# A two-block layer kernel on one core: a reordered start, with small first loads, eight alternating conversions and splits, and the norm's sum one slot later

## The chip, the cores and the metric

The kernel runs on one core of a Trainium2 chip. The metric is device time in microseconds (us) of one execution. A launch computes two neural layers, one after the other, for 256 positions with 2048 channels, all in 32-bit floating point.

## What is computed

The first block is a hybrid layer (attention and a state-space branch side by side, then a gated feed-forward part); the second is another hybrid layer with adaptive modulation. What matters for this change is the beginning of the first block:

```
def rms_norm(x, w):
    xf = x.astype(jnp.float32)
    y = xf * lax.rsqrt(jnp.mean(xf * xf, axis=-1, keepdims=True) + EPS)
    return (y * w.astype(jnp.float32)).astype(x.dtype)

def hybrid_layer(x, norm1_w, w_in, ...):
    h = rms_norm(x, norm1_w)
    proj = h @ w_in
    q, k, v, z, xbc, dt_raw = jnp.split(proj, SPLIT_POINTS, axis=-1)
    ...
    xbc = jax.nn.silu(causal_dwconv(xbc, ssm_conv_w, ssm_conv_b))
    dt = jax.nn.softplus(dt_raw.astype(jnp.float32) + dt_bias.astype(jnp.float32))
```

The kernel does not divide by the root of the mean before the product. It multiplies `X * norm1_w` by `w_in`, and the reciprocal root, one number for each position, is applied to the product afterwards. So the norm's sum of squares is not needed before the first group of output columns is finished.

## The kernel before

**Products.** Each 32-bit product is made of three TensorE passes in a reduced type: both operands are split into a high part (a rounded copy) and a low part (the remainder), and `hi*hi + hi*lo + lo*hi` is accumulated. For the activations `X` the parts are `gh` and `gl`; for the weights they are `whi` and `wlo`. ScalarE (ACT) makes the high parts, VectorE (DVE) the low parts.

**Units and slots.** The weights come as 528 units of 512 KB, each two contraction tiles by 512 output columns. A unit is loaded by the SyncE (SP) queue into one of `RAW = 8` buffers `raw`, `split(blk, j)` on ACT copies it to one of `SPLIT = 4` buffers `whi`, `split` on DVE subtracts it into `wlo`, and TensorE (PE) spends 24 matmuls of 256 columns on it (8 tiles by 3 passes). Eight units make one group of 512 output columns. The first projection `B_IN` has 88 units. Its main loop counts slots n = 0 to 87: in slot n, PE multiplies unit n, while ACT and DVE run `split(B_IN, LEAD + n)` with `LEAD = 4`, four units ahead, and then `slot1(n)`, which holds all the other work of that slot.

**The waits of a split.** `split` on ACT waits for the unit's load (`s_raw`) and until PE has finished the unit four earlier (`s_used`), because there are four `whi` buffers. `split` on DVE waits for `whi` (`s_hi`). PE waits for `wlo` (`s_lo`). SP refills a `raw` buffer when DVE has split it (`s_lo`).

**Before slot 0.** SP issues five parts of `X` (256, 256, 512, 512, 512 KB) alternating with units 0 to 4, then units 5 to 7. ACT issues the parameter table `prm` (553 columns) and the constants `cst` (ones, identity, triangle), and then, for each of eight steps u, converts two tiles of `X` (`gh`, scaled by `norm1`), and for u below 4 also splits unit u. DVE follows with `gl` and `wlo`. ACT issues `wdt` (the weights of dt) after step 1 and `mask` after step 2. PE runs 13 matmuls on zeroed data, which touch no result, and then starts unit 0 when `wlo` of it is there.

**The norm's sum.** In slots 0 to 3, `squares` on ACT squares four tiles of `X` each, into two buffers; `sum_chunk` on DVE adds the second buffer into the first, so the third and the fourth square wait for the addition before them (`s_sum`). `fold` adds the four tiles to one. In slot 7 PE sums over the channels (`sum_squares`), ACT takes the root (`root`), DVE its reciprocal (`inverse_root`), and DVE scales the first finished group out of PSUM (`ssm_evac`). Slots 8 to 14 then hold the convolution of that group: a base on ACT (`ssm_base`), three taps on DVE for each of four tiles (`ssm_taps`), and `ssm_silu` on ACT. Slots 10 to 22 hold also the steps of dt (`dt_steps`), whose last product on PE is in slot 22.

Of the kernel before, what the change touches and what calls it, by code (L numbers as in the profile page):

```python
# [18 lines left out]
ACT = mybir.ActivationFunctionType  # L19
AX_X = mybir.AxisListType.X  # L20

P = 128
# [43 lines left out]


GAINS = (15, 17, 18, 19, 20, 21, 22, 23, 25, 26, 27, 28)
FINAL = ((4, 1), (5, 1), (6, 2), (8, 2), (10, 2))
# [13 lines left out]
def build(nc, xT, weights, w_dt, w_ada, c_rows, params, const1, const2, rows, outT):  # L83
    ctx = ExitStack()
    with ctx:
# [162 lines left out]
        s_inv, s_rq, s_kb, s_rqc = sem("s_inv"), sem("s_rq"), sem("s_kb"), sem("s_rqc")  # L248
        s_rcl = sem("s_rcl")
        s_tile, s_part = sem("s_tile"), sem("s_part")  # L250
        s_fold, s_own, s_near, s_far = sem("s_fold"), sem("s_own"), sem("s_near"), sem("s_far")
# [53 lines left out]
        def _(act):  # L305
# [54 lines left out]

            act.dma_start(prm[:, :], params).then_inc(s_prm, 16)
            act.dma_start(cst[:, :], const1[:, 0:3 * P + 32]).then_inc(s_cst, 16)
            act.wait_ge(s_prm, 16)
            act.activation(small[:, 240:241], col("eps"), ACT.Copy).then_inc(s_warm, 1)

            for u in range(DT // 2):
                for c in range(len(X_PARTS)):
                    if X_PARTS[c][0] == 2 * u:
                        act.wait_ge(s_x[c], 16)
                for t in (2 * u, 2 * u + 1):  # L370
                    act.activation(gh[:, t, :], X[:, t, :], ACT.Copy, scale=col("norm1", t)).then_inc(s_gh, 1)
                if u < 4:
                    split(B_IN, u)
                if u == 1:
                    act.dma_start(wdt[:, :, :], w_dt).then_inc(s_wdt, 16)
                if u == 2:
                    act.dma_start(mask[:, :], const1[:, 3 * P + 32:]).then_inc(s_mask, 16)
# [77 lines left out]
            def slot1(n):  # L455
                if n < 4:
                    squares(0, n, SQX1)
                if n == 7:
                    root(0, D)
                g, j = n // 8 - 1, n % 8  # L460
                if 0 <= g < 3:
                    if j < 4:
                        ssm_base(g, j)
                    if j == 6:
                        ssm_silu(g)
# [43 lines left out]
                attention_slot(n, ATT0, 0, 8, 0)  # L509

            for n in range(IN_SLOTS):
                split(B_IN, LEAD + n)
                slot1(n)
# [145 lines left out]
        def _(dve):  # L659
# [71 lines left out]
            for u in range(DT // 2):  # L731
                for t in (2 * u, 2 * u + 1):
                    dve.wait_ge(s_gh, t + 1)
                    dve.scalar_tensor_tensor(gl[:, t, :], X[:, t, :], col("norm1", t), gh[:, t, :].bitcast(F32),
                                             ALU.mult, ALU.subtract).then_inc(s_gl, 1)
                if u < 4:
                    split(B_IN, u)
            dve.memset(U[:, :, 0:3], 0.0).then_inc(s_ready, 1)
# [225 lines left out]
            def slot1(n):  # L964
# [4 lines left out]
                if n == 5:  # L969
                    dve.wait_ge(s_wdt, 16)  # L970
                    dve.tensor_tensor(wdt[:, :, :], wdt[:, :, :], col("norm1", 0, DT).unsqueeze(2).to_broadcast([P, DT, 32]),
                                      ALU.mult).then_inc(s_wdtn, 1)
                g, j = n // 8 - 1, n % 8
                if 0 <= g < 3 and 1 <= j < 5:
                    ssm_taps(g, j - 1)
                dt_steps(n)
# [41 lines left out]
            for n in range(IN_SLOTS):  # L1018
                split(B_IN, LEAD + n)
                if n == 64:  # L1020
                    dve.wait_ge(s_mask, 16)
                if n == 7:
                    inverse_root(0)
                    dve.wait_ge(s_rb, 1)
                    dve.wait_ge(s_ready, 1)
                if n % 8 == 7:
                    if n < 24:
                        ssm_evac(n // 8)
                    else:
                        land(n // 8)  # L1030
                slot1(n)
# [263 lines left out]
        def _(pe):  # L1295
            def product(b, out, tiles, first, last, hi, lo, apart=False, ready=None):
# [14 lines left out]
                mm.then_inc(s_used, 1)  # L1311

            def product_high_first(out, need):

# [86 lines left out]
            def stream_in(blk, grp, n, need):  # L1401

                g, u = n // 8, n % 8
                if u == 0:
                    pe.wait_ge(s_evac, grp + g + 1)
                pe.wait_ge(s_lo, 8 * blk + n + 1)
                if g in (NAT if blk == B_IN else NAT2):
                    product_nat(n % SPLIT, (grp + g) % 2, (2 * u, 2 * u + 1), u == 0, u == 7)
                    return
                if blk == B_IN2 and n == 0:  # L1410
                    product_high_first(acc_tiles(grp % 2), need)
                    return
                product(n % SPLIT, acc_tiles((grp + g) % 2), (2 * u, 2 * u + 1), u == 0, u == 7, gh, gl,
                        ready=need if g == 0 else None)
# [18 lines left out]
            pe.wait_ge(s_zero, 1)  # L1433
            for _ in range(13):
                pe.matmul(PS[:, 7, 0:S], VS1[:, 0, 0, :], VS1[:, 0, :, :], start=True, stop=True)
# [90 lines left out]
            def slot1(n):  # L1526
                if n == 7:
                    pe.wait_ge(s_cst, 16)
                    sum_squares(0, SQX1)
# [249 lines left out]
```

## Time and profile before

| | |
|---|---|
| time, median of 3 runs | 1556.51 us (1551.45 to 1557.78) |
| profiled execution, its own time | 1558.2 us |
| span of the profiled execution | 1556.5 us |
| PE busy | 1542.8 us (99%) |
| PE weight loads busy | 1501.8 us (96%) |
| DVE busy | 1136.7 us (73%) |
| ACT busy | 779.7 us (50%) |
| mean granted TensorE clock | 0.995 |

The own time of the profiled execution is 1.7 us over its span; the span is counted from the first to the last instruction. Times in the rows are microseconds from the start of the span. The rows that the prediction reads are in the section below.

### The profile page before, as it was taken

Reading aid. Unit: us, or ns where it says so; the run is one execution under the profiler, and the core shown is the slowest. Engines: PE = TensorE matmul, PEld = TensorE weight load, DVE = VectorE, ACT = ScalarE, POOL = GpSimd, SP = SyncE. Lnnn points to the kernel's source line nnn. Section 1 sums busy time; section 2 is a strip of 40 time slices with the busy share of each in tenths; the row PEclk is TensorE's granted clock in tenths of the full one; section 3 lists DMA queues with packets and bytes.
Section 4 is the critical chain, followed back from the end, with each engine's and each line's share of the span. In section 5 each row is a group of like instructions: output and inputs, shape, how many; then the busy total and the mean of one; then the engine's idle time right before and its main releaser. Section 6 shows DMA issues by size and latency. Waiting matters only on the chain.

```text
span 1556.5 us, 32067 instructions
## 1 busy us (share of the span) xinstructions
PE 1542.8 (99%) x12598; PEld 1501.8 (96%) x12598; DVE 1136.7 (73%) x1373; ACT 779.7 (50%) x931; POOL 29.7 (2%) x56
## 2 busy tenths in 40 slices
PE   9999999999999999999999999999999999999997
PEld 9999997999999999999999999999999989999997
DVE  7867767758888878888788888879754644764755
ACT  6545445544554445444444444545554643454544
POOL 0000000000000000000000000000000000000000
PEclk9999999999999999999999999999999999999999
DMA  9464546447777767677686776866465554445451
GB/s 346 165 253 155 202 163 224 156 161 273 291 252 258 277 220 299 229 268 269 220 302 223 269 269 228 296 219 217 145 243 190 181 190 160 160 163 178 161 183 62
DMA packets 85793, 339.31 MB, mean 218 GB/s; under 512 B 9536, under 2 KB 10064, under 8 KB 79184
## 3 DMA queue, kind: packets, MB, share of 16 engines
q1 hardware_dynamic: 77760, 281.05, 50.7%
q0 software_dynamic: 7232, 54.55, 9.7%
q10 hardware_dynamic: 720, 2.53, 0.5%
q8 instruction: 63, 1.03, 0.3%
q14 instruction: 18, 0.15, 0.0%
HBM read 335.97 MB, written 2.12 MB: 217 GB/s over the span
## 4 chain that ended last, share of the span: by engine, by line
PE 93%; DVE 4%; ACT 1%; issue 1%; DMA 1%; SPq 0%; DVEq 0%; ACTq 0%
PE PS L1305 27%; PE PS L1307 26%; PE PS L1309 26%; PE PS L1336 3%; PE PS L1335 3%; PE PS L1333 3%; DVE wlo L672 1%; PE PS L1500 1%; PE PS L1479 1%; DMA raw<-weights 1%; ACT whi L318 1%; PE PS L1675 0%; DVE HRT L882 0%; PE PS L1462 0%; DVE conv_acc L753 0%
## 5 line engine op out<-in xcount | busy, mean ns | idle before, releaser
L672 DVE TENSOR_TENSOR wlo<-raw,whi 128x1024 fp32r<-128x1024 f32 x528 | 643.2, 1222 | 363.7 <-ACT whi L318 360.0
L318 ACT ACTIVATE whi<-raw 128x1024 fp32r<-128x1024 f32 x528 | 557.5, 1059 | 664.0 <-PE PS L1309 589.9
L1305 PE MATMUL PS<-gh,whi 128*128 128x256 f32 x3112 | 873.4, 281 | 0.1
L1307 PE MATMUL PS<-gl,whi 128*128 128x256 f32 x3112 | 866.0, 278 | 0.0
L1309 PE MATMUL PS<-gh,wlo 128*128 128x256 f32 x3112 | 865.9, 278 | 0.0
L1305 PEld LDWEIGHTS PS<-gh,whi 128*128 128x128 f32 x3112 | 589.2, 189 | 4.6 <-DVE wlo L672 1.9
L1307 PEld LDWEIGHTS PS<-gl,whi 128*128 128x128 f32 x3112 | 585.3, 188 | 0.9
L1309 PEld LDWEIGHTS PS<-gh,wlo 128*128 128x128 f32 x3112 | 585.5, 188 | 0.0
L1305 PE MATMUL PS<-ah,whi 128*128 128x256 f32 x688 | 190.1, 276 | 0.0
L1309 PE MATMUL PS<-ah,wlo 128*128 128x256 f32 x688 | 189.9, 276 | 0.0
L1307 PE MATMUL PS<-al,whi 128*128 128x256 f32 x688 | 189.9, 276 | 0.0
L1307 PEld LDWEIGHTS PS<-al,whi 128*128 128x128 f32 x688 | 129.1, 188 | 0.0
L1305 PEld LDWEIGHTS PS<-ah,whi 128*128 128x128 f32 x688 | 129.1, 188 | 0.0
L1309 PEld LDWEIGHTS PS<-ah,wlo 128*128 128x128 f32 x688 | 129.1, 188 | 0.0
L1099 DVE SCALAR_TENSOR_TENSOR ada_w<-ada_w,c_act 128x2048 f32<-128x2048 f32 x40 | 91.4, 2285 | 0.0
L1333 PE MATMUL PS<-whi,gh 128*128 128x512 f32 x192 | 77.4, 403 | 0.0
L1336 PE MATMUL PS<-wlo,gh 128*128 128x512 f32 x192 | 75.7, 394 | 0.0
L1335 PE MATMUL PS<-whi,gl 128*128 128x512 f32 x192 | 75.6, 394 | 0.0
L688 DVE TENSOR_TENSOR X<-PS,X 128x1024 f32<-128x1024 f32 x47 | 57.2, 1217 | 0.0
L1333 PEld LDWEIGHTS PS<-whi,gh 128*128 128x128 f32 x192 | 36.2, 188 | 8.7 <-issue 0.8
L1336 PEld LDWEIGHTS PS<-wlo,gh 128*128 128x128 f32 x192 | 36.1, 188 | 8.0
L1335 PEld LDWEIGHTS PS<-whi,gl 128*128 128x128 f32 x192 | 36.2, 188 | 7.9
(249 smaller groups left out, 890.4 us busy)
## 6 DMA issues: line engine op xcount, KB each, us to landing
raw<-weights SPq DMA_DIRECT2D x528, 512.0 KB, 3.4
ada_w<-w_ada POOLq DMA_DIRECT2D x48, 1024.0 KB, 6.2
EM<-rows POOLq DMA_DIRECT2D x1, 3072.0 KB, 11.7
X<-xT SPq DMA_DIRECT2D x3, 512.0 KB, 8.8
c<-const ACTq DMA_DIRECT2D x1, 1536.0 KB, 7.1
c_act<-c_rows POOLq DMA_DIRECT2D x1, 1024.0 KB, 6.7
outT<-X SPq DMA_DIRECT2D x2, 512.0 KB, 3.2
outT<-X SPq DMA_DIRECT2D x3, 256.0 KB, 2.2
```

The source lines that it names most:

```text
L318: act.activation(whi[:, j % SPLIT, :], raw[:, j, :], ACT.Copy).then_inc(s_hi, 1)
L672: dve.tensor_tensor(wlo[:, j % SPLIT, :], raw[:, j, :], whi[:, j % SPLIT, :].bitcast(F32), ALU.subtract).then_inc(s_lo, 1)
L688: dve.tensor_tensor(x, acc_tiles(par), x, ALU.add).then_inc(s_evac, 1)
L1099: dve.scalar_tensor_tensor(w, w, 1.0, c_act[:, :], ALU.mult, ALU.mult, accum_out=modT[:, bass.ds(i * ADA_STEP + (ADA_FIRST - ADA_STEP + k) ...
L1305: pe.matmul(out[:, t, :], whi[:, b, w], hi[:, kt, :], start=first and half == 0 and (apart or t % 2 == 0), stop=False, skip_group_check=True)
L1307: pe.matmul(out[:, t, :], whi[:, b, w], lo[:, kt, :], start=False, stop=False, skip_group_check=True)
L1309: mm = pe.matmul(out[:, t, :], wlo[:, b, w], hi[:, kt, :], start=False, stop=last and half == 1, skip_group_check=True)
L1333: pe.matmul(out, gh[:, kt, m], whi[:, b, w], start=first and half == 0, stop=False, skip_group_check=True)
L1335: pe.matmul(out, gl[:, kt, m], whi[:, b, w], start=False, stop=False, skip_group_check=True)
L1336: mm = pe.matmul(out, gh[:, kt, m], wlo[:, b, w], start=False, stop=last and half == 1, skip_group_check=True)
L1479: mm = pe.matmul(PS[:, 4, at:at + keys], q[:, P * c:P * c + P], k[:, 0:keys], start=True, stop=True)
L1500: mm = pe.matmul(PS[:, 6, first:S], v(b, P * (h % 4)), PTS[:, h % 2, b, 0:S - first], start=(b == 1), stop=(b == 0), skip_group_check=True)
```

## The change

The change touches the first 15 slots or so:

- **Loads.** Ahead of everything ACT now requests only the first 16 columns of the parameter table (`norm1`). The other 537 columns are requested in step 3, `cst` in step 4, `mask` in step 5, and `wdt` in step 2 in place of step 1. ACT and DVE wait for the second part of the table (`s_prm2`) after the eight steps.
- **Conversions and splits.** The eight steps now each convert two tiles of `X` and split one unit, so that units 0 to 7 are split before slot 0. The first four slots hold no split any more.
- **PE.** There are 7 of the matmuls on zeroed data in place of 13. Units 0 and 1 go through `product_first`: it needs only the high weights for its first 16 matmuls, and the low weights for its last 8.
- **Slots.** The norm's sum, root and reciprocal and the first `ssm_evac` go from slot 7 to slot 8. The base and the taps of the first convolution group start one slot later; those of the other groups stay.

```
@@ scalar @@
-            act.dma_start(prm[:, :], params).then_inc(s_prm, 16)
-            act.dma_start(cst[:, :], const1[:, 0:3 * P + 32]).then_inc(s_cst, 16)
+            act.dma_start(prm[:, 0:DT], params[:, 0:DT]).then_inc(s_prm, 16)
             act.wait_ge(s_prm, 16)
-            act.activation(small[:, 240:241], col("eps"), ACT.Copy).then_inc(s_warm, 1)
+            act.activation(small[:, 240:241], prm[:, 0:1], ACT.Copy).then_inc(s_warm, 1)
...
-                if u < 4:
-                    split(B_IN, u)
-                if u == 1:
+                split(B_IN, u)
+                if u == 2:
                     act.dma_start(wdt[:, :, :], w_dt).then_inc(s_wdt, 16)
-                if u == 2:
+                if u == 3:
+                    act.dma_start(prm[:, DT:], params[:, DT:]).then_inc(s_prm2, 16)
+                if u == 4:
+                    act.dma_start(cst[:, :], const1[:, 0:3 * P + 32]).then_inc(s_cst, 16)
+                if u == 5:
                     act.dma_start(mask[:, :], const1[:, 3 * P + 32:]).then_inc(s_mask, 16)
...
-                if n == 7:
+                if n == 8:
                     root(0, D)
-                g, j = n // 8 - 1, n % 8
-                if 0 <= g < 3:
-                    if j < 4:
+                for g in range(3):
+                    j = n - 8 * g - (8 if g else 9)
+                    if 0 <= j < 4:
                         ssm_base(g, j)
...
+            act.wait_ge(s_prm2, 16)
             for n in range(IN_SLOTS):
-                split(B_IN, LEAD + n)
+                if n >= DT // 2 - LEAD:
+                    split(B_IN, LEAD + n)
                 slot1(n)
@@ vector @@
-                if u < 4:
-                    split(B_IN, u)
+                split(B_IN, u)
+            dve.wait_ge(s_prm2, 16)
...
-                g, j = n // 8 - 1, n % 8
-                if 0 <= g < 3 and 1 <= j < 5:
-                    ssm_taps(g, j - 1)
+                for g in range(3):
+                    j = n - 8 * g - (9 if g else 10)
+                    if 0 <= j < 4:
+                        ssm_taps(g, j)
...
-                split(B_IN, LEAD + n)
+                if n >= DT // 2 - LEAD:
+                    split(B_IN, LEAD + n)
...
-                if n == 7:
+                if n == 8:
                     inverse_root(0)
                     dve.wait_ge(s_rb, 1)
                     dve.wait_ge(s_ready, 1)
-                if n % 8 == 7:
+                    ssm_evac(0)
+                if n % 8 == 7 and n > 7:
@@ tensor @@
+            def product_first(n, out):
+
+                pe.wait_ge(s_hi, n + 1)
+                for kt in (2 * n, 2 * n + 1):
+                    for x, signal in ((gh, s_gh), (gl, s_gl)):
+                        pe.wait_ge(signal, kt + 1)
+                        for t in range(4):
+                            at = 512 * (kt % 2) + P * t
+                            pe.matmul(out[:, t, :], whi[:, n, at:at + P], x[:, kt, :],
+                                      start=kt == 0 and x is gh and t % 2 == 0, stop=False, skip_group_check=True)
+                pe.wait_ge(s_lo, n + 1)
+                for kt in (2 * n, 2 * n + 1):
+                    for t in range(4):
+                        at = 512 * (kt % 2) + P * t
+                        mm = pe.matmul(out[:, t, :], wlo[:, n, at:at + P], gh[:, kt, :], start=False, stop=False,
+                                       skip_group_check=True)
+                mm.then_inc(s_used, 1)
...
+                if blk == B_IN and n < FIRST:
+                    product_first(n, acc_tiles(grp % 2))
+                    return
...
-            for _ in range(13):
+            for _ in range(7):
...
-                if n == 7:
+                if n == 8:
                     pe.wait_ge(s_cst, 16)
                     sum_squares(0, SQX1)
```

The first place is ACT around the end of the eight steps. `gh` is a conversion, `whi` a split, and `SQX_73` the buffers of the squares. Before, from the split of unit 4 on:

```order
L318 ACTIVATE whi<-raw 128x1024 [waits s_used,s_raw4]
L333 ACTIVATE SQX_73<-X 128x1024
L318 ACTIVATE whi<-raw 128x1024 [waits s_used,s_raw5]
L333 ACTIVATE SQX_73<-X 128x1024
L318 ACTIVATE whi<-raw 128x1024 [waits s_used,s_raw6]
L333 ACTIVATE SQX_73<-X 128x1024 [waits s_sum]
L318 ACTIVATE whi<-raw 128x1024 [waits s_used,s_raw7]
L333 ACTIVATE SQX_73<-X 128x1024 [waits s_sum]
L318 ACTIVATE whi<-raw 128x1024 [waits s_used,s_raw0]
```

And now, on the same engine, from the same split:

```order
L320 ACTIVATE whi<-raw 128x1024 [waits s_used,s_raw4]
L379 DMA cst<-const 128x416
L372 ACTIVATE gh<-X,prm 128x256 x2
L320 ACTIVATE whi<-raw 128x1024 [waits s_used,s_raw5]
L381 DMA mask<-const 128x384
L372 ACTIVATE gh<-X,prm 128x256 [waits s_x4]
L372 ACTIVATE gh<-X,prm 128x256
L320 ACTIVATE whi<-raw 128x1024 [waits s_used,s_raw6]
L372 ACTIVATE gh<-X,prm 128x256 x2
L320 ACTIVATE whi<-raw 128x1024 [waits s_used,s_raw7]
L335 ACTIVATE SQX_73<-X 128x1024 [waits s_prm2]
L335 ACTIVATE SQX_73<-X 128x1024
```

The four squares, which stood one behind each of the splits of units 4 to 7, now all stand behind the split of unit 7, and ahead of the split of unit 8 (the next that waits for `s_raw0`).

The second place is DVE at the same point. `SQX_73<-SQX_73` are the three additions of `sum_chunk` (128x1024) and the two of `fold`. Before, from the split of unit 6:

```order
L672 TENSOR_TENSOR wlo<-raw,whi 128x1024 [waits s_hi]
L701 TENSOR_TENSOR SQX_73<-SQX_73 128x1024 [waits s_sum,s_sq]
L672 TENSOR_TENSOR wlo<-raw,whi 128x1024 [waits s_hi]
L701 TENSOR_TENSOR SQX_73<-SQX_73 128x1024 [waits s_sum,s_sq]
L706 TENSOR_TENSOR SQX_73<-SQX_73 128x512 [waits s_sum]
L707 TENSOR_TENSOR SQX_73<-SQX_73 128x256 [waits s_dve]
L672 TENSOR_TENSOR wlo<-raw,whi 128x1024 [waits s_hi] x2
```

And now, from the split of unit 7:

```order
L678 TENSOR_TENSOR wlo<-raw,whi 128x1024 [waits s_hi]
L744 MEMSET U 128x12x3 [waits s_prm2]
L707 TENSOR_TENSOR SQX_73<-SQX_73 128x1024 [waits s_sq]
L707 TENSOR_TENSOR SQX_73<-SQX_73 128x1024 [waits s_sum,s_sq] x2
L712 TENSOR_TENSOR SQX_73<-SQX_73 128x512 [waits s_sum]
L713 TENSOR_TENSOR SQX_73<-SQX_73 128x256 [waits s_dve]
L678 TENSOR_TENSOR wlo<-raw,whi 128x1024 [waits s_hi] x2
```

All three additions and both steps of the fold now stand between the split of unit 7 and that of unit 8.

The third place is DVE in slot 13, where the first steps of dt stand (`DTW` is their buffer, `conv_acc` that of the taps). Before:

```order
L672 TENSOR_TENSOR wlo<-raw,whi 128x1024 [waits s_hi]
L785 TENSOR_SCALAR DTW<-PS,prm 32x256 [waits s_ready,s_dtc]
L787 COPY DTW<-prm 128x8
L788 SCALAR_TENSOR_TENSOR DTW<-DTW 128x264 [waits s_dve]
L672 TENSOR_TENSOR wlo<-raw,whi 128x1024 [waits s_hi]
```

And now:

```order
L678 TENSOR_TENSOR wlo<-raw,whi 128x1024 [waits s_hi]
L759 SCALAR_TENSOR_TENSOR conv_acc<-U,prm,conv_acc 128x256 [waits s_base]
L759 SCALAR_TENSOR_TENSOR conv_acc<-U,prm,conv_acc 128x256 [waits s_tap] x2
L791 TENSOR_SCALAR DTW<-PS,prm 32x256 [waits s_ready,s_dtc]
L793 COPY DTW<-prm 128x8
L794 SCALAR_TENSOR_TENSOR DTW<-DTW 128x264 [waits s_dve]
```

Three taps of the first group now stand in slot 13 ahead of the dt steps; they stood in slot 12.

## Rows read from the trace of the kernel before

**Rows 1.** Timeline of PE and its weight loads (PEld): start, duration, what [idle before, releaser].

```profile
1.43 8.24 PE L1435 MATMUL PS<-VS 128*128 128x256 f32 x26 [1.43 <-DVE VS L728]
...
9.32 0.47 PE L1305 MATMUL PS<-gh,whi 128*128 128x256 f32 x1
...
21.12 0.19 PEld L1305 LDWEIGHTS PS<-gh,whi 128*128 128x128 f32 x1 [0.35 <-DVE wlo L672]
...
32.42 0.31 PEld L1431 LDWEIGHTS PS<-SQX,cst 128*128 128x128 f32 x2
32.76 0.19 PEld L1305 LDWEIGHTS PS<-gh,whi 128*128 128x128 f32 x1
...
79.09 0.52 PEld L1550 LDWEIGHTS PS<-small,cst 128*128 128x128 f32 x4 [0.78 <-DVE small L812]
```

**Rows 2.** Timeline of ACT, 4 to 28 us, same columns.

```profile
4.99 0.20 ACT L364 ACTIVATE small<-prm 128x1 f32<-128x1 f32 x1 [1.89 <-DMA prm<-params]
...
6.85 1.06 ACT L318 ACTIVATE whi<-raw 128x1024 fp32r<-128x1024 f32 x1 [0.86 <-DMA raw<-weights]
...
14.44 1.06 ACT L318 ACTIVATE whi<-raw 128x1024 fp32r<-128x1024 f32 x1 [1.07 <-DMA raw<-weights]
15.40 3.30 ACT L371 ACTIVATE gh<-X,prm 128x256 fp32r<-128x256 f32 x8
...
26.33 1.07 ACT L333 ACTIVATE SQX<-X 128x1024 f32<-128x1024 f32 x1 [0.34 <-DVE SQX L701]
```

**Rows 3.** The load of unit 7: its issue, and its time to landing.

```profile
L264 SPq DMA_DIRECT2D raw<-weights x1: 434/434/434, 7.0 to 7.0; - x1
...
DMA to landing us min/median/max: 15.8/15.8/15.8
```

**Rows 4.** DMA issues on the ACT queue, 0 to 40 us: count, KB each, us to landing.

```profile
prm<-params ACTq DMA_DIRECT2D x1, 276.5 KB, 4.1
wdt<-w_dt ACTq DMA_DIRECT2D x1, 256.0 KB, 6.2
cst<-const ACTq DMA_DIRECT2D x1, 208.0 KB, 5.7
mask<-const ACTq DMA_DIRECT2D x1, 192.0 KB, 6.3
```

**Rows 5.** The issue of `wdt`, and all packets of 7.2 to 12.3 us by queue (q1 SP's, q10 ACT's).

```profile
8.95 0.33 ACTq L375 DMA_DIRECT2D wdt<-w_dt  x1
...
q1 hardware_dynamic: 580, 2.11, 102.7%
```

**Rows 6.** Stretches: length, busy of PE, PEld, DVE, ACT, POOL, granted clock, DMA, GB/s.

```profile
6.00:30.00 24.00, 23.85 (x188) 23.18 (x187) 20.52 (x31) 19.68 (x29) 0.00 (x0) 1.00 1.03 411
81.30:84.80 3.50, 3.50 (x19) 3.50 (x18) 0.01 (x1) 1.16 (x3) 0.68 (x1) 0.51 0.80 269
84.80:88.20 3.40, 3.40 (x32) 3.40 (x31) 1.56 (x2) 1.06 (x1) 0.56 (x1) 1.00 0.46 155
```

**Rows 7.** Timeline of DVE, 26 to 33 us: additions of the norm's sum and the next splits.

```profile
27.43 1.23 DVE L701 TENSOR_TENSOR SQX<-SQX 128x1024 f32<-128x1024 f32 x1
28.69 0.69 DVE L706 TENSOR_TENSOR SQX<-SQX 128x512 f32<-128x512 f32 x1
29.41 0.43 DVE L707 TENSOR_TENSOR SQX<-SQX 128x256 f32<-128x256 f32 x1
29.76 2.36 DVE L672 TENSOR_TENSOR wlo<-raw,whi 128x1024 fp32r<-128x1024 f32 x2
```

**Rows 8.** Timeline of DVE, slots 12 to 15.

```profile
51.47 1.52 DVE L753 SCALAR_TENSOR_TENSOR conv_acc<-U,prm,conv_acc 128x256 f32<-128x256 f32 x3
...
57.60 1.23 DVE L672 TENSOR_TENSOR wlo<-raw,whi 128x1024 fp32r<-128x1024 f32 x1 [1.53 <-ACT whi L318]
...
62.73 1.23 DVE L672 TENSOR_TENSOR wlo<-raw,whi 128x1024 fp32r<-128x1024 f32 x1 [1.06 <-ACT whi L318]
```

More of the change, by code:

```diff
@@ L64, in head_tile @@
     return low + h if h < 4 else high + h - 4
+FIRST = 2
 GAINS = (15, 17, 18, 19, 20, 21, 22, 23, 25, 26, 27, 28)
@@ L249, in build @@
         s_rcl = sem("s_rcl")
+        s_prm2 = sem("s_prm2")
         s_tile, s_part = sem("s_tile"), sem("s_part")
```

## The prediction

> **What bounds the kernel now.** I read the shares of busy time first, then the timelines of PE, ACT and DVE for the first 90 us, then the DMA views of the same stretch. PE is busy for 99% of the span, and its weight loads for 96%. From its first product at 9.32 us on it waits rarely, and the reader should see in [rows 1] how little is open to this change: 9.3 us before the first product, one wait of 0.35 us before unit 4, and one of 0.78 us in slot 22, where PE waits for the dt steps. The rest of the program is TensorE work that the change leaves alone. The pace of PE is in the same rows: units 4 to 7 run from 21.12 to 32.42, so one unit takes 11.30/4 = 2.83 us.
>
> The second thing to see is that PE's pace is not the tightest one at the start. The DMA engines are full: 411 GB/s from 6 to 30 us at a share of 1.03 [rows 6]. A unit of 512 KB is 0.524 MB and takes 1.28 us. ACT waits for loads up to unit 3 at 14.44 us, and the load of unit 7, issued at 7.0, lands 15.8 us later, at 22.8 us [rows 2, 3]. Before the change that is early enough, because the squares of the norm are made between the splits while those loads arrive.
>
> **The start.** In front of unit 0, ACT's queue now carries 8 KB (16 columns) in place of 276.5 + 208 KB [rows 4]. The 476.5 KB less are 0.488 MB, or 1.19 us at the rate of [rows 6]. Unit 0, which ACT began to copy at 6.85 us [rows 2], is there at about 5.7 us, its high part 1.06 us later, at 6.8. A transfer of 64-byte rows is not in the trace; the parameters of 276.5 KB landed 4.1 us after their issue, and I take no more than that for the small one, so it does not come last. The 26 records of the work on zeros took 8.24 us [rows 1]; 14 records take 4.4 us at their mean, more if the slow ones are all at the front, so they end between 5.9 and 7.4 us. The product no longer waits for the low part. I let PE start at 7.0 us, 2.3 earlier. Units 0 to 7 then end at 7.0 + 8 x 2.83 = 29.6 us, if nothing holds them: each copy follows its load, and the low part of unit 4, which PE waits for first, comes at about the time that PE reaches it, 18.3 us.
>
> **What takes the gain away.** The 2.3 us are worth something only if unit 8 is split by 29.6 us. Its split now stands on both engines behind the whole norm's sum, and that behind the split of unit 7, as the first two places of the order show. So I follow this chain.
>
> Step one is when ACT begins to split unit 7; call it s. Four causes compete. (a) PE has to be done with unit 3: 7.0 + 11.3 = 18.3. (b) ACT's own pace: a copy takes 0.96 (14.44 to 15.40) and two conversions 3.30/4 = 0.83 [rows 2], so 1.79 a unit; unit 3's load, 1.19 earlier than 14.44, is there at 13.25, and four units on it is 20.4. (c) The load of unit 7, with all the late requests behind it: the bytes ahead shrink by `wdt`, parameters, `cst` and `mask`, 924.5 KB or 2.3 us, so 22.8 - 2.3 = 20.5. (d) The same load with all of them ahead: then exactly the same bytes precede it as before, and it lands at 22.8. The requests leave ACT at the splits of units 2 to 5, some 10.5 to 18 us, and those of before landed 6.2 to 6.3 us after their issue [rows 4]. That puts the first three ahead of unit 7 and `mask`, 192 KB or 0.48 us, partly behind it. I take s = 22.6, with the bounds 20.5 and 22.8.
>
> Here a rule can be held against a row. `wdt` was issued on ACT's queue at 8.95, but from 7.2 to 12.3 us only packets of SP's queue moved [rows 5]; a request behind SP's backlog waits for a part of it. The Trainium skill (DMA: Bandwidth & Descriptors, "Queues, rings and completion order") says that each DMA engine takes turns between the queues that have work. By it `mask` too would move at once and s be 22.8; by the row it moves last, and s is 22.3.
>
> Step two is the chain behind s. The first two squares start 0.96 and 1.92 later, and the second takes 1.07, to s + 3.0. The first addition takes 1.23, the third square 1.07, the second addition 1.23 [rows 2, 7]: s + 6.5. From the start of the fourth square to the start of the next low split the trace has 29.76 - 26.33 = 3.43 us [rows 2, 7], with the third addition and both steps of the fold in it, and the low split takes 2.36/2 = 1.18. Together s + 11.1, and with some 0.04 us for each of five hand-offs s + 11.3. Unit 8 starts at 22.6 + 11.3 = 33.9 us, between 31.8 and 34.1. PE, done with unit 7 at 29.6, is idle for 4.3 us. Behind the DVE's split of unit 8 stand those of 9, 10 and 11, at 1.2 to 1.9 us each; PE needs 2.83 for a unit, so they are not late again. The root, the reciprocal and the first evacuation, one slot on, keep their distance to PE, and group 2, which needs the evacuated bank, comes eight slots later.
>
> **The sum.** Before, unit 8 started at 32.76 with the norm's sum on PE (32.42 to 32.76, 0.34 us) behind it [rows 1]; now that sum still follows. The first term is 33.9 + 0.34 - 32.76 = +1.5 us, with the bounds -0.6 and +1.7.
>
> The second term is the clock. At 79.09 PE had waited 0.78 us and then ran small matmuls, and from 81.3 to 84.8 the granted clock is 0.51, the lower level, 1.2 of 2.4 GHz: 19 matmuls in 3.5 us, where the next 3.4 us at the full clock hold 32 [rows 1, 6]. At that pace 3.5 us would hold 33, so the stretch lost 14/33 of 3.5, or 1.5 us. An idle time of 4.3 us before unit 8 should bring on the same. I add 1.5; the bounds are 0 and, for two such stretches, 3.0.
>
> The third term is slot 13. Three taps, 1.52 us, now stand ahead of the dt steps, on whose end PE waited 0.78 us in slot 22. DVE waited for ACT for 1.53 and 1.06 us in the two slots behind them [rows 8]. The dt steps and ACT's exponential behind them move as one, but those pauses can take up most of it. I take +0.3, between 0 and 1.5.
>
> Edits at no cost: the high-first order of units 0 and 1 has the same 24 matmuls each. The second wait for parameters stands behind unit 7's split at 23.6 us; the request leaves ACT near 13.5 and at 6.3 us, as `mask` took, is there by 19.8. Uncovered it would cost one for one. `cst` is needed in slot 8, at 37 us, `wdt` in slot 5, `mask` in slot 64.
>
> The sum is 1.5 + 1.5 + 0.3 = +3.3 us. On the profiled execution's own time, 1558.2 us, that is 1561.5. That execution stands 1.7 us above the median of the runs, 1556.51, so the time to expect of a median is 1559.8 us, 0.2% more. A measurement of this kernel tells about 0.5%, or 7.8 us, from no change; this is no change that it can tell.
>
> **Rivals.**
>
> - *The loads come in time.* If unit 7's load does not decide, s is 18.3 by cause (a), unit 8 can start at 29.6, just as PE gets there, and the first term is 29.6 + 0.34 - 32.76 = -2.8 us, with no loss of clock: -2.5 in all, 1554.0 us. For it speaks that the early start is real. Against it, ACT's own pace (b) forbids an s below 20.4 even with no late request ahead, and the full DMA engines leave no room to catch up.
> - *The gap costs its length and nothing more.* The wait comes as forecast, but the clock stays up, or the low clock that followed slot 22 in the trace (1.5 us) does not come this time and pays for the new one. Then +1.8, 1558.3 us. For it: the low stretch at 81.3 followed a thin one by little, and a shift may miss it. Against: 4.3 us without work is much more than the 0.78 us seen ahead of that fall.
> - *Slower: the second part of the parameters is late.* It stands on ACT in front of the first square. From a landing of 23.6 us on, each us late is a us lost. To be over 7.8 us slower with the other terms it must land after 23.6 + 4.5 = 28.1, 14.6 us behind its request; for 9 us it is 1565.5. For it: requests on ACT's queue waited behind SP's backlog, and a unit's load took 15.8 us [rows 3]. Against: none on ACT's queue took over 6.3 us.
>
> **Chances and range.** The forecast has 0.58; the gap without the clock's price 0.22; loads in time 0.12; the late parameters 0.04; others, of either sign, 0.04. The bounds of the terms give -0.6 to +6.2 us, or 1555.9 to 1562.7. The first rival takes the low end to 1554.0, and for the runs, which lie up to 5 us from their median, I add about 1 at the top: 1554.0 to 1563.5 holds over 8 in 10. Faster by over 0.5% would need 7.8 us out of a start that has 9.3 in all: 0.02. Slower by over 0.5%: 0.04. Within 0.5%: 0.94.
>
> **What would show it.** PE's first product at about 7.0 us; unit 7's load landing at 22 to 23; ACT's four squares behind its split; a wait of PE for `wlo` of about 4 us that ends near 33.9; then a stretch of granted clock near 0.5; the dt matmuls of slot 22 waiting about 1 us. The prediction is wrong if unit 8 starts before 31.8 us, if unit 4, 5 or 6 holds PE up by more than the slack before unit 8, or if a wait that this trace doesn't have stands behind slot 8.

## The result and the profile after

The changed kernel takes 1560.34 us in the median of 20 runs (1554.6 to 1572.87), the kernel before 1555.56 us in 20 runs beside them (1550.08 to 1557.89). The ratio is 1.0034, with a 95% interval of 1.0021 to 1.0046: 3 to 7 us slower, within the 0.5% that was taken as the bound of no change. The profiled execution has a span of 1552.9 us and an own time of 1554.6 us, less than that of before; why one profile can be faster while the median is slower is told at the end. A few executions of several kernels, and a third of those in the last set (covered22_again, covered_both and covered_plain, with before beside them), took 13 to 25 us longer than the others; the medians of that set are over the runs under 1560 us.

TensorE (PE) and its weight loads (PEld), as in [rows 1]: start, duration, what, and in brackets the idle time before and its releaser.

```profile
1.43 4.70 PE L1465 MATMUL PS<-VS 128*128 128x256 f32 x14 [1.43 <-DVE VS L734]
...
6.92 0.53 PEld L1330 LDWEIGHTS PS<-gh,whi 128*128 128x128 f32 x4 [1.20 <-issue]
...
33.43 0.29 PEld L1314 LDWEIGHTS PS<-gh,whi 128*128 128x128 f32 x1 [4.01 <-issue]
38.50 0.31 PEld L1461 LDWEIGHTS PS<-SQX,cst 128*128 128x128 f32 x2
...
82.86 0.52 PEld L1580 LDWEIGHTS PS<-small,cst 128*128 128x128 f32 x4 [1.19 <-DVE small L818]
```

PE starts 2.4 us earlier, runs units 0 to 7 without a break, and then (at 29.42) stands still for 4.01 us before unit 8, which starts at 33.43, 0.67 us later than before. The 38.50 row, the norm's sum behind unit 8, shows the second cost: unit 8 took 5.1 us and not 2.8.

The timeline of ACT, beside [rows 2]:

```profile
12.95 1.06 ACT L320 ACTIVATE whi<-raw 128x1024 fp32r<-128x1024 f32 x1 [0.69 <-DMA raw<-weights]
...
16.08 1.06 ACT L320 ACTIVATE whi<-raw 128x1024 fp32r<-128x1024 f32 x1 [1.26 <-DMA raw<-weights]
...
20.33 1.06 ACT L320 ACTIVATE whi<-raw 128x1024 fp32r<-128x1024 f32 x1 [0.64 <-DMA raw<-weights]
21.30 0.89 ACT L372 ACTIVATE gh<-X,prm 128x256 fp32r<-128x256 f32 x2
22.09 1.04 ACT L320 ACTIVATE whi<-raw 128x1024 fp32r<-128x1024 f32 x1
23.04 1.99 ACT L335 ACTIVATE SQX<-X 128x1024 f32<-128x1024 f32 x2
26.33 1.06 ACT L335 ACTIVATE SQX<-X 128x1024 f32<-128x1024 f32 x1 [1.29 <-DVE SQX L707]
28.68 1.06 ACT L335 ACTIVATE SQX<-X 128x1024 f32<-128x1024 f32 x1 [1.29 <-DVE SQX L707]
29.64 3.88 ACT L320 ACTIVATE whi<-raw 128x1024 fp32r<-128x1024 f32 x4
```

And of DVE, beside [rows 7]:

```profile
25.07 1.23 DVE L707 TENSOR_TENSOR SQX<-SQX 128x1024 f32<-128x1024 f32 x1 [0.44 <-ACT SQX L335]
27.42 1.23 DVE L707 TENSOR_TENSOR SQX<-SQX 128x1024 f32<-128x1024 f32 x1 [1.13 <-ACT SQX L335]
29.77 1.23 DVE L707 TENSOR_TENSOR SQX<-SQX 128x1024 f32<-128x1024 f32 x1 [1.12 <-ACT SQX L335]
31.03 0.69 DVE L712 TENSOR_TENSOR SQX<-SQX 128x512 f32<-128x512 f32 x1
31.76 0.43 DVE L713 TENSOR_TENSOR SQX<-SQX 128x256 f32<-128x256 f32 x1
32.10 2.35 DVE L678 TENSOR_TENSOR wlo<-raw,whi 128x1024 fp32r<-128x1024 f32 x2
```

The two timelines interlock like a zip: the third square waits for the first addition, the second addition for the third square, and so on, each pause over 1.1 us. From the split of unit 7 (22.09) to PE's start on unit 8 (33.43) it is 11.34 us. The row at 20.33 shows where this begins: ACT waited 0.64 us there for the load of unit 6, and split unit 7 right behind the next two conversions.

The load of unit 7, beside [rows 3], and the requests on ACT's queue, beside [rows 4]:

```profile
L266 SPq DMA_DIRECT2D raw<-weights x1: 432/432/432, 6.9 to 6.9; - x1
...
DMA to landing us min/median/max: 15.1/15.1/15.1
```

```profile
prm<-params ACTq DMA_DIRECT2D x1, 268.5 KB, 7.6
wdt<-w_dt ACTq DMA_DIRECT2D x1, 256.0 KB, 6.4
cst<-const ACTq DMA_DIRECT2D x1, 208.0 KB, 6.8
mask<-const ACTq DMA_DIRECT2D x1, 192.0 KB, 7.1
prm<-params ACTq DMA_DIRECT2D x1, 8.0 KB, 3.8
```

Unit 7 landed at 22.0 us, 0.8 us earlier than before. The small first load took 3.8 us for 8 KB, hardly less than the 4.1 us of the whole table.

Busy times in stretches, in the columns of [rows 6]:

```profile
6.00:29.60 23.60, 22.78 (x193) 22.23 (x192) 17.97 (x26) 17.64 (x26) 0.00 (x0) 1.00 1.03 410
29.60:33.40 3.80, 0.03 (x1) 0.00 (x0) 3.56 (x5) 3.80 (x5) 0.00 (x0) 0.77 0.40 161
33.40:38.40 5.00, 4.94 (x23) 4.97 (x24) 4.15 (x5) 0.12 (x1) 0.00 (x0) 0.50 0.71 215
```

After the idle stretch the granted clock is 0.50, the lower level, for all of unit 8: 23 matmuls in 5.0 us. At 0.118 us each, the pace of units 4 to 7 before, they would have taken 2.7 us, so the low clock cost 2.3 us. It fell within the idle time, near 31.6 us, and was down for about 7 us, of which PE worked 5.0.

### The profile page after: what moved, and what is told of

Its sections match the earlier page's. It is cut to its first block, busy times and chain, and to the rows that moved or that the text cites. A ratio compares the mean times of both kernels' runs of the same rounds, so it can differ in the third digit from the quotient of the medians.

```text
span 1552.9 us, 32043 instructions
## 1 busy us (share of the span) xinstructions
PE 1534.6 (99%) x12586; PEld 1494.3 (96%) x12586; DVE 1137.0 (73%) x1373; ACT 778.6 (50%) x930; POOL 29.8 (2%) x56
## 4 chain that ended last, share of the span: by engine, by line
PE 92%; DVE 4%; ACT 1%; issue 1%; DMA 1%; SPq 0%; DVEq 0%; ACTq 0%
PE PS L1314 26%; PE PS L1318 26%; PE PS L1316 26%; PE PS L1363 3%; PE PS L1362 3%; PE PS L1360 3%; DVE wlo L678 1%; DMA raw<-weights 1%; PE PS L1530 1%; PE PS L1509 1%; ACT whi L320 1%; PE PS L1705 0%; DVE HRT L888 0%; DVE conv_acc L759 0%; PE PS L1492 0%
```

## The experiments

Three places serve to compare the traces up to a point: the start of the dt product of slot 9 (32 records on PE), the start of the first transposes of slot 25, and the start of the first column sums at the norm between the two blocks. All in us from the start of the span:

| kernel | PE's idle before unit 8 | dt product | transposes | second norm | span of the profile |
|---|---|---|---|---|---|
| before | none | 38.52 | 90.73 | 1108.58 | 1556.5 |
| changed | 4.01 | 41.88 | 92.89 | 1110.77 | 1552.9 |
| warm13 | 1.39 | 39.27 | 90.56 | 1108.53 | 1557.7 |
| filler | 0.36 | 39.57 | 92.17 | 1110.00 | 1557.2 |
| no_alternation | none | 37.27 | 88.28 | 1106.09 | 1548.8 |
| squares_between | none | 35.95 | 88.49 | 1106.02 | 1549.8 |
| taps_back | 3.84 | 41.98 | 92.88 | 1110.73 | 1559.9 |
| full_first | 3.94 | 42.06 | 95.80 | 1114.03 | 1561.4 |
| alternation_only | 0.84 | 40.53 | 92.30 | 1111.07 | 1559.7 |
| covered22 | none | 36.59 | 87.64 | 1105.57 | 1553.6 |
| covered22_again | none | 35.71 | 86.76 | 1104.61 | 1553.8 |
| covered_both | none | 36.53 | 87.59 | 1105.51 | 1549.0 |
| covered_plain | none | 37.45 | 88.50 | 1107.20 | 1549.1 |

The column of the spans does not follow the one before it: from the second norm to the end a profile takes either 442 to 444 us or 447 to 449. That part is the same code in all of them, so the theories are judged by the middle columns, and the medians are given beside them.

**warm13: the later start back.**

```
-            for _ in range(7):
+            for _ in range(13):
```

> The changed kernel with 13 matmuls on zeros again in place of 7, so that TensorE starts about 2.4 us later, at 9.3 us. Theory (the chain of the norm's sum decides when unit 8 starts): unit 8 starts at 33.4 us as in the changed kernel, the idle time before it shrinks from 4.0 to about 1.6 us, and the whole time is the same or up to 2.3 us less, by as much of the low-clock stretch as goes. Rival (the early start is worth its time): unit 8 starts near 35.8 us and the kernel takes 2.4 us more.

```profile
33.16 0.19 PEld L1314 LDWEIGHTS PS<-gh,whi 128*128 128x128 f32 x1 [1.39 <-issue]
35.88 0.30 PEld L1461 LDWEIGHTS PS<-SQX,cst 128*128 128x128 f32 x2
```

Unit 8 starts at 33.16 us, though PE started its work 2.4 us later, and takes 2.7 us (to the sum at 35.88) in place of 5.1: no stretch at the low clock. The dt product is 2.6 us earlier than in the changed kernel. The rival, that the early start is worth its time, is out: in this order of work the early start only lengthened the idle time, and the clock fell behind it. Median 1559.54 against 1557.07 of before (ratio 1.0010, 0.9989 to 1.0031).

**filler: work in the gap.**

```
             for n in range(IN_SLOTS):
+                if n == 8:
+                    for _ in range(9):
+                        pe.matmul(PS[:, 7, 0:S], VS1[:, 0, 0, :], VS1[:, 0, :, :], start=True, stop=True)
                 stream_in(B_IN, G_IN, n, lambda kt: kt + 1)
```

> The changed kernel with 9 matmuls on zeros between units 7 and 8 (3.8 us of TensorE work in the idle time of 4.0 us). Theory (the idle time costs twice, by its length and by the lower clock after it): unit 8 still starts at 33.4 to 33.8 us, no stretch at the lower clock stands behind it, and the dt product of slot 9 comes 2.3 us earlier. Rival (the clock falls for another reason, or costs nothing because another engine binds there): the stretch stays, or goes without any gain in time.

```profile
33.46 0.19 PEld L1314 LDWEIGHTS PS<-gh,whi 128*128 128x128 f32 x1 [0.36 <-issue]
```

Unit 8 starts where it did, and the dt product comes at 39.57, 2.3 us earlier than in the changed kernel. The granted clock is 1.00 from 33 to 36 us. So the low clock is a price of its own, of 2.3 us, and the idle time brings it on. Later the profile lost most of this again: it had a stretch at the low clock from about 82.5 to 86 us, behind slot 22, and its transposes are only 0.7 us ahead of the changed kernel's. Median 1559.52 against 1557.07 (ratio 1.0006, 0.9985 to 1.0027).

**no_alternation: units 4 to 7 in the slots again.**

```
-                split(B_IN, u)
+                if u < 4:
+                    split(B_IN, u)
...
-            act.wait_ge(s_prm2, 16)
             for n in range(IN_SLOTS):
-                if n >= DT // 2 - LEAD:
-                    split(B_IN, LEAD + n)
+                split(B_IN, LEAD + n)
+                if n == 6:
+                    act.wait_ge(s_prm2, 16)
```

The same on DVE.

> The changed kernel without the alternation: units 4 to 7 are split in slots 0 to 3 with a square between each, as before; the small first load, the late requests, the high-first units, the 7 matmuls on zeros and the sum in slot 8 stay, and the wait for the second part of the parameters stands in slot 6. Theory (the squares behind unit 7's split make the loss): the idle time before unit 8 goes, one of about 1.6 us comes before unit 4, unit 8 starts near 31.2 us, and the kernel is 4 to 5 us faster than the changed one and about 1 us faster than before. Rival (the late requests or the sum's slot make the loss): unit 8 stays near 33 us and the time within 1 us of the changed kernel.

```profile
20.26 0.19 PEld L1316 LDWEIGHTS PS<-gh,whi 128*128 128x128 f32 x1 [1.36 <-DVE wlo L679]
33.88 0.30 PEld L1463 LDWEIGHTS PS<-SQX,cst 128*128 128x128 f32 x2
```

The idle time of 4.0 us is gone, one of 1.36 us stands before unit 4, the norm's sum comes at 33.88, which puts the start of unit 8 near 31.1, and the dt product is 4.6 us earlier than in the changed kernel and 1.25 us earlier than before. Everything else of the change is still in: the late requests and the sum's later slot are not the loss. Median 1553.90 against 1557.07 (ratio 0.9979, 0.9959 to 1.0000); the last section tells why this is more than the 1.25 us.

**squares_between: the alternation kept, the squares between the splits.**

```
                 split(B_IN, u)
+                if u >= 4:
+                    squares(0, u - 4, SQX1)
...
                 split(B_IN, u)
+                if u in (5, 6):
+                    sum_chunk(0, u - 4, SQX1)
...
-                if 1 <= n < 4:
-                    sum_chunk(0, n, SQX1)
-                if n == 3:
-                    fold(0, 3, SQX1)
+                if n == 4:
+                    sum_chunk(0, 3, SQX1)
+                    fold(0, 3, SQX1)
```

> The changed kernel with each square of the norm behind the split of units 4 to 7 inside the eight steps, the first two additions in steps 5 and 6, and the third addition with the fold behind the split of unit 8. Theory: unit 8's low part is ready at about 28.6 us, TensorE waits under 1 us before unit 7 and not before unit 8, unit 8 starts near 30.2 us without a low-clock stretch, and the kernel is about 5.5 us faster than the changed one and 1 to 2.5 us faster than before. Rival (the loads bind: with full DMA engines no order of ACT helps): unit 8 still starts after 32.5 us.

```profile
26.91 0.19 PEld L1315 LDWEIGHTS PS<-gh,whi 128*128 128x128 f32 x1 [0.17 <-DVE wlo L678]
32.56 0.31 PEld L1462 LDWEIGHTS PS<-SQX,cst 128*128 128x128 f32 x2
```

PE waits 0.17 us before unit 7 and is through unit 8 at 32.56, 5.9 us earlier than the changed kernel. The loads, which are the same, allow this, so they do not hold unit 8 to 33.4 us; the order of the squares does. The dt product is 2.6 us earlier than before, by the transposes of slot 25 it is 2.2: this profile had a low clock near 78 us, as before had at 81.3. Median 1555.59 against 1557.07 (ratio 0.9982, 0.9961 to 1.0002).

**taps_back: the first group's convolution one slot earlier.**

```
-                    j = n - 8 * g - (8 if g else 9)
+                    j = n - 8 * g - 8
...
-                    j = n - 8 * g - (9 if g else 10)
+                    j = n - 8 * g - 9
```

> The changed kernel with the base and the taps of the first convolution group one slot earlier, where they stood before; the norm's sum stays in slot 8. Theory (three taps ahead of the dt steps lengthen the wait of slot 22): up to unit 13 nothing changes, unit 8 starts at 33.4 us after 4.0 us of idle time, and the wait of slot 22 is 0.8 us again in place of 1.2, so the kernel is 0.4 us faster than the changed one. Rival (that wait follows from the late start of the first evacuation): it stays at 1.2 us.

PE waited 0.8 us in slot 22 in place of 1.2, as the theory has it. It did not show in the time: the transposes of slot 25 start at 92.88, against 92.89, and the second norm at 1110.73, against 1110.77. The start was 0.1 us later, and the rest went in small differences of pace. The taps are not all that sets this wait: alternation_only, which has them where they stood before, waited 1.35 us there. Median 1560.55 against 1556.39 (ratio 1.0024, 1.0012 to 1.0037).

**full_first: the whole table and the constants ahead again.**

```
-            act.dma_start(prm[:, 0:DT], params[:, 0:DT]).then_inc(s_prm, 16)
+            act.dma_start(prm[:, :], params).then_inc(s_prm, 16)
+            act.dma_start(cst[:, :], const1[:, 0:3 * P + 32]).then_inc(s_cst, 16)
```

The two late requests go, and the second waits are on `s_prm`.

> The changed kernel with the whole parameter table and the constants requested ahead of everything again, as before the change; all else is as changed. Theory (the same bytes stand ahead of unit 7 either way): TensorE starts about 1.1 us later, at 8 us, the split of unit 7 begins at 22.1 to 22.9 us, unit 8 starts between 33.4 and 34.2 us, and the time is within 1 us of the changed kernel. Rival (the small first load is worth its 1.2 us to the end): unit 8 starts at 34.6 us or later.

```profile
34.21 0.19 PEld L1311 LDWEIGHTS PS<-gh,whi 128*128 128x128 f32 x1 [3.94 <-issue]
```

Unit 8 starts at 34.21, 0.8 us later than in the changed kernel: the upper end of what the theory gave, and under the rival's 34.6. So the theory that the first load is worth nothing is too strong: PE started 0.8 us later and so did unit 8, some 0.8 of the 1.2 us of the small load. Beyond that the profile had a wait of 1.75 us in slot 22, for which I have no test. Median 1561.76 against 1556.39 (ratio 1.0031, 1.0009 to 1.0052).

**alternation_only: one part of the change, on the kernel before.** The edit is the alternation alone, the reverse of no_alternation, without the later parameters.

> The kernel before with one part of the change: the eight steps each split one unit and the first four slots split none. Loads, 13 matmuls on zeros, unit order and the sum in slot 7 are as before. Theory: TensorE starts at 9.3 us, the split of unit 7 begins near 22.9 us, when its load has landed, the chain of 11.3 us puts unit 8 at 34.0 us in place of 32.8, and the kernel is 1.0 to 1.5 us slower than before in the trace up to slot 9. Rival (the alternation helps, by taking away the wait before unit 4): it is 0.4 us faster.

```profile
33.55 0.30 PEld L1431 LDWEIGHTS PS<-SQX,cst 128*128 128x128 f32 x2 [0.95 <-issue]
34.68 0.19 PEld L1305 LDWEIGHTS PS<-gh,whi 128*128 128x128 f32 x1 [0.84 <-issue]
```

PE now waits first for the fold (0.95 us) and then for unit 8's low part (0.84). Unit 8 starts at 34.68, and the dt product 2.0 us later than before, more than the 1.0 to 1.5 expected and of the same sign; PE started at 9.84 and not 9.3, and the chain began at 23.34 and not 22.9. It took 11.34 us, as in the changed kernel; taps_back, full_first and warm13 have 11.34, 11.34 and 11.36. The median is 1559.12 against 1556.39 (ratio 1.0020, 1.0006 to 1.0035). This one part makes a kernel slower that has none of the others.

**covered22, covered22_again, covered_both, covered_plain: work in PE's waits.** covered22 is squares_between with the taps back and three matmuls on constants in slot 22:

```
                 if n == 22:
+                    idle(3)
                     pe.wait_ge(s_dts, 2)
```

covered_both adds five more at the norm between the blocks, and covered_plain has both of these edits and the taps on no_alternation:

```
+                if k == 2:
+                    pe.wait_ge(s_tile, 1)
+                    idle(2)
...
+                if k == 2:
+                    idle(3)
                 pe.wait_ge(s_icol, k - 1)
```

> The kernel squares_between, with the base and the taps of the first group one slot earlier, and three matmuls on constants on TensorE in slot 22, ahead of its wait for the dt steps (1.28 us of work in an idle time of 0.8 to 1.2 us). Theory (idle time is what brings the clock down there): no idle time in slot 22, no low-clock stretch near 80 us, and unit 28 is reached within 0.5 us of where squares_between would reach it without its low stretch: 1 to 3 us faster than before in the median. Rival (the thin matmuls of slot 22 alone bring it down): a low stretch of 3.4 us still follows in some profiles.

> The kernel covered22 once more, beside the two below on the same chip. Theory: its start is about 3 us ahead of before's (unit 28 reached near 86.3 us), whatever pace TensorE falls into later; the median is 1 to 4 us under before's. Rival (the early units' gain is lost later): unit 28 is early, but unit 384 is reached no earlier than before.

> covered22 with five more matmuls on constants at the norm between the two blocks (near 1107 us): two ahead of the wait for the squares, three ahead of the wait for the reciprocal root. Theory (idle time and thin matmuls bring the clock down there too): the low-clock stretch near 1110 us, which stood in all ten profiles so far, goes or is put off, and the kernel is 1 to 2 us faster than covered22. Rival (the thin single-column matmuls alone bring it down): the stretch stays and the five matmuls cost up to 1 us. Second question: whether TensorE's pace from unit 400 to 450, 113 or 118 ns a matmul in the profiles so far, still differs from run to run.

> no_alternation with the base and taps one slot earlier, the three matmuls in slot 22, and the five at the second norm. Theory: unit 8 starts near 31.1 us, 1 us later than in covered_both; the median is within 1.5 us of covered_both and 1 to 3 us under before. Rival (the alternation is worth keeping): covered_both is faster by more than 2 us.

In no profile of the four did PE wait in slot 22, and none had a low clock near 80 us; of the nine others five had. covered22 reaches the second norm at 1105.57 and 1104.61 us in its two profiles, 3.0 and 4.0 us ahead of before. Its medians are 1554.94 against 1556.39 (ratio 0.9998, 0.9976 to 1.0021) and 1554.73 against 1556.44 (0.9991, 0.9946 to 1.0035): the right sign, and not shown by the intervals. covered_both had a low clock at the second norm in its profile all the same, so work in the gaps does not always prevent it there. Its five executions under 1560 us have a median of 1550.0; its ratio, 1.0016 (0.9975 to 1.0058), tells nothing. covered_plain had no low clock there, and is the one version whose interval lies wholly under 1: a median of 1550.74 over seven runs against 1556.44, ratio 0.9973, 0.9957 to 0.9990. That is 5.7 us where 1 to 3 were expected, and its trace is only 1.4 us ahead of before at the second norm. Most of the difference is not shown to come from the edit, as the last section tells. It keeps the small first load and the early start, and not the alternation. That the alternation would be worth keeping has no support: covered_both is not faster than covered_plain by these runs, within 1.5 us, as expected.

## Why the prediction was right

**The start.** PE was to start at 7.0 us and did at 6.92. The load of unit 0 was to be there at 5.7 and was; ACT copied it at 5.80 and came straight from its conversions, which the small table, landed at 4.7, had let start at 4.82. So both bound the start, and a slower small table would have come last. Nothing held PE before unit 8, as forecast.

**The gain taken away.** The chain behind the split of unit 7 was to take 11.3 us and took 11.34. It was to begin at 22.6 and began at 22.09, within the bounds of 20.5 to 22.8; this is what made the first term +1.5 where the rows give 33.43 + 0.31 - 32.76 = +1.0. The cause was none of the four as priced. Cause (b) took ACT's pace from unit 3 on and gave 20.4, but ACT waited for loads twice more, 1.26 us for unit 4 and 0.64 for unit 6, which it split at 20.33. Unit 7's split came 1.76 us behind that, and its own load was down at 22.0, almost at the same time. So the loads set the base, as causes (c) and (d) have it, by unit 6's as much as by unit 7's. `mask`, issued at 17.68, landed last, at 24.8, 2.8 us behind unit 7, as the row had said.

As for the rule held against the row: `wdt`, issued at 10.41, had moved one packet by 14.0 us, and from 14 to 16 the two queues moved side by side, ACT's packets for 32.9% of the engines' time and SP's for 71.3%. So a request of ACT's waited for a part of SP's backlog, and only then took turns with it. The second half agrees with the Trainium skill (DMA: Bandwidth & Descriptors, "Queues, rings and completion order"), by which the engines take turns between the queues; for when a request begins to move, the row was the better guide.

**The clock.** It was to cost 1.5 us and cost 2.3: 5.0 us of PE's work at the low level, not 3.5. The bounds of 0 to 3.0 held it. This is the term of the sum that was missed most. filler and warm13 show that it follows from the idle time. The Trainium skill (TensorE: Matmul & The Clock Gate, "HAM oscillation — how this bites in real kernels") warns of waits that send the engine back to the low clock; the trace agrees, with 0.50 granted behind 4.01 us of idle time. The length of a wait alone does not tell it, though: in slot 22, where small matmuls follow the wait, the clock fell in five profiles of nine, behind 0.78, 1.17, 1.18, 1.35 and 1.75 us, and stayed up in four behind 0.77, 1.17, 1.18 and 1.19.

**Slot 13.** +0.3 was expected; the wait of slot 22 grew from 0.78 to 1.19, or +0.4, and taps_back put it back to 0.8. alternation_only shows that something else moves this wait as well; what, is open.

**The sum.** The terms come to 1.0 + 2.3 + 0.4 = +3.7 in the trace, against +3.3: the first was 0.5 too high and the clock 0.8 too low, and that they cancel is luck. The dt product, ahead of slot 22, is 3.36 us later. The median moved by 4.8 us, the ratio says 5.3 with an interval of 3 to 7. What is over the 3.7 lies within that interval; it is not explained by a step of its own. That the median itself, 1560.34, is so near to the 1559.8 of the forecast is luck too: the median of before was 1556.51 in the 3 runs that the forecast started from, and 1555.56 in the 20 beside the changed kernel.

**The rivals.** "The loads come in time" asked for s = 18.3, and s was 22.09. But the argument against it, that the full DMA engines leave no room to catch up, holds for this order only: squares_between reaches unit 8 near 29.7 us with the same loads. "The gap costs its length and nothing more" happened by half in the profiled run: the new low clock came, the old one at 81.3 us did not, and by the transposes of slot 25 the changed kernel is only 2.2 us behind. Whether the old one comes differs from profile to profile, so this half is no effect of the change that could be shown. The late parameters did not come: their second part landed 7.6 us after its issue at 12.96, at 20.6, 2.4 us ahead of the first square. None of the signs of being wrong came.

## What to carry to other kernels

A start that is made earlier gains only as much as the next thing that the bound engine needs comes earlier too: follow the chain behind the last moved instruction, on every engine that it crosses, to the place where the bound engine picks it up. Work that goes back and forth between two engines (square, add, square, add) adds up its latencies when it stands alone, 11.3 us here; in squares_between, with splits and conversions between, PE waited 0.17 us. Moving the work between away exposes them. And an idle time of TensorE can cost more than its length, because the clock can come back low: 4.01 us of waiting cost 2.3 us more.

## What the runs showed of the hardware

TensorE has two paces at the same granted clock. From 1160 to 1200 us every kernel runs the same product loop at the full clock; the first row is of the kernel before, the second of the changed one (length, PE busy with its count, granted clock, DMA share, GB/s).

```profile
1160.00:1200.00 40.00, 40.00 (x342) 1.00 0.56 190
```

```profile
1160.00:1200.00 40.00, 40.00 (x355) 1.00 0.59 198
```

That is 117 or 113 ns for a matmul of 256 columns. Eight of the thirteen profiles have 342 there and five 355 or 356. From 600 to 640 us all thirteen have 355 or 356. From the second norm to the end the changed kernel's profile takes 5.8 us less than that of before, on equal code, and this is why this one profile has the shorter span though the median is longer. The runs of before alone lie in two groups to match, 9 of 20 between 1550 and 1553 us and 11 between 1555 and 1558. Those of the changed kernel do so too, 5 of 20 between 1554 and 1556 and 15 from 1558 on. Group against group, the medians of the changed kernel are 4.7 and 4.2 us longer, so its loss does not come from the mixture.

For the small gains the mixture matters. In the lower group (under 1554 us) lie 6 of 12 runs of no_alternation against 6 of 35 of before, and 6 of the 7 runs under 1560 us of covered_plain against 4 of 22. Within the lower group covered_plain has a median of 1550.42 against 1551.59, or 1.2 us less, and in the upper it has a single run, 1.6 us less; the 5.7 us between the medians are mostly the mixture. Whether an edit can move a run from one group to the other is open. The two kernels with five matmuls more at the second norm have 11 of their 12 runs under 1560 us in the lower group, covered22 has 7 of 19; but only 12 of the 24 runs of those two are under 1560 us, and covered22's two profiles have the slower pace (x342) as before has. What sets the pace was not tried. For a kernel like this it means that single profiles can't be compared by their spans, only up to a common place, and medians of few runs only with an eye on the groups.
